# Three rounded products with the values, a second exponential on ScalarE, and a new order around the latent attention

## The reference, cut to what matters

```python
def mla_mixer(q_c, kv_c, k_r, pos, g_q, w_uq, g_kv, w_ukv):
    q = (rms_norm(q_c, g_q) @ w_uq).reshape(b, s, MLA_HEADS, MLA_QK)
    q = jnp.concatenate([q[..., :MLA_NOPE], rotary(q[..., MLA_NOPE:], pos)], -1)
    kv = (rms_norm(kv_c, g_kv) @ w_ukv).reshape(b, s, MLA_HEADS, MLA_NOPE + MLA_V)
    k_nope, v = kv[..., :MLA_NOPE], kv[..., MLA_NOPE:]
    ...
    return causal_block_attention(q, k, v)

def one_block(args):                      # inside causal_block_attention
    sc = jnp.einsum('bhqd,bhkd->bhqk', q_blk, kt, preferred_element_type=jnp.float32) * scale
    p = jax.nn.softmax(jnp.where(mask, sc, -jnp.inf), axis=-1)
    return jnp.einsum('bhqk,bhkd->bhqd', p.astype(vt.dtype), vt)
...
    a = mla_mixer(...)                    # in first_block
    r = retention_mixer(...)
    y = jnp.concatenate([a, r], axis=-1) @ w_out[l]
```

## Time and profile before

| | us |
|---|---|
| median of three runs | 2687.31 (2684.17 to 2688.14) |
| the profiled execution, its own time | 2691.6 |
| its span in the profile | 2689.8 |
| PE busy in the span | 2504.4 (93%) |
| DVE, ACT, POOL busy | 1350.4, 651.6, 733.9 |

### The profile page before, as it was taken

One profiled execution on the slowest core, in us unless ns is written; L12 is line 12 of the kernel. 1 busy time (PEld: TensorE's weight loads), 2 busy tenths in 40 slices (PEclk: granted clock), 3 DMA queues, 4 the chain that ended last, 5 costly groups with the idle time before them and its releaser, 6 DMA issues.

```text
span 2689.8 us, 29003 instructions
## 1 busy us (share of the span) xinstructions
PE 2504.4 (93%) x11544; PEld 1955.2 (73%) x11544; DVE 1350.4 (50%) x1513; ACT 651.6 (24%) x946; POOL 733.9 (27%) x490
## 2 busy tenths in 40 slices
PE   5998779989999999999998689999998999999998
PEld 3776556657678888888886368886586778888877
DVE  7556743434643444444435779996528321314433
ACT  3002224431432001101123421113204200025521
POOL 1241320015463332332345211210045223330011
PEclk9999879999999999999999899999999999979999
DMA  6651000022132332332222121112232521110021
GB/s 225 198 164 61 20 18 8 8 95 86 58 107 83 94 98 75 94 98 87 79 85 79 39 94 41 35 39 102 69 123 82 163 74 47 47 40 1 1 86 71
DMA packets 228851, 206.96 MB, mean 77 GB/s; under 512 B 15248, under 2 KB 203280, under 8 KB 227712
## 3 DMA queue, kind: packets, MB, share of 16 engines
q1 hardware_dynamic: 223552, 178.61, 21.9%
q10 hardware_dynamic: 3840, 21.89, 2.1%
q0 software_dynamic: 1344, 4.91, 0.5%
HBM read 180.35 MB, written 17.83 MB: 74 GB/s over the span
## 4 chain that ended last, share of the span: by engine, by line
PE 78%; DVE 9%; ACT 4%; issue 4%; PEld 2%; POOL 1%; DMA 1%; PEldq 1%; ACTq 0%; DVEq 0%; SPq 0%; POOLq 0%
PE G L1633 28%; PE G L304 25%; PE G L1099 2%; PE M L3001 2%; PE M L307 2%; PE G L2506 1%; PE M L400 1%; PE M L1649 1%; PE G L2322 1%; PE M L2322 1%; PE M L2986 1%; PE M L1010 1%; DVE WMAX L3024 1%; PE G L2349 1%; PE M L2508 1%
## 5 line engine op out<-in xcount | busy, mean ns | idle before, releaser
L278 POOL TENSOR_SCALAR WH<-RAW 128x1024 fp32r<-128x1024 f32 (+1 forms) x154 | 134.2, 872 | 887.2 <-PE G L1633 515.5
L304 PE MATMUL G<-HH,WH 128*128 128x512 f32 x1056 | 336.8, 400 | 14.5 <-POOL WL L2164 7.8
L304 PE MATMUL G<-HH,WL 128*128 128x512 f32 x1056 | 332.5, 396 | 0.0
L304 PE MATMUL G<-HL,WH 128*128 128x512 f32 x1056 | 332.4, 396 | 0.0
L281 POOL TENSOR_TENSOR WL<-RAW,WH 128x1024 fp32r<-128x1024 f32 (+1 forms) x154 | 299.4, 1944 | 12.9
L1633 PE MATMUL G<-HH,WH 128*128 128x512 f32 x640 | 227.2, 404 | 13.3 <-POOL WL L281 8.5
L304 PEld LDWEIGHTS G<-HH,WH 128*128 128x128 f32 x1056 | 188.2, 189 | 61.4 <-issue 19.2
L1633 PE MATMUL G<-HH,WL 128*128 128x512 f32 x640 | 223.8, 398 | 0.0
L1633 PE MATMUL G<-HL,WH 128*128 128x512 f32 x640 | 223.7, 398 | 0.0
L304 PEld LDWEIGHTS G<-HL,WH 128*128 128x128 f32 x1056 | 188.7, 188 | 42.2
L304 PEld LDWEIGHTS G<-HH,WL 128*128 128x128 f32 x1056 | 188.5, 188 | 42.1
(11 more groups left out here) (536 smaller groups left out, 4445.2 us busy)
## 6 DMA issues: line engine op xcount, KB each, us to landing
RAW<-in_w_ff SPq DMA_DIRECT2D x40, 512.0 KB, 3.8
RAW<-in_w_ff SPq DMA_DIRECT2D x80, 256.0 KB, 2.8
WVEC<-in_w_ada SPq DMA_DIRECT2D x24, 512.0 KB, 4.6
FVEC<-in_e_w_mod SPq DMA_DIRECT2D x24, 512.0 KB, 3.8
FVEC<-in_o_w_mod SPq DMA_DIRECT2D x24, 512.0 KB, 3.6
RAW<-in_o_w_in SPq DMA_DIRECT2D x24, 512.0 KB, 3.6
RAW<-in_e_w_in SPq DMA_DIRECT2D x20, 512.0 KB, 3.6
ADA<-in_w_ada SPq DMA_DIRECT2D x4, 2048.0 KB, 19.5
```

What stands on the lines that cost most here:

```text
L278: pool.tensor_scalar(hi, raw, 1.0, 0.0, ALU.mult, ALU.add).then_inc(w_high, 1)
L304: m = pe.matmul(G[s][:, n * w:(n + 1) * w], part[s][:, k, :], acts[i][:, k, n * w:(n + 1) * w], start=first, stop=last)
```

## The change

In the stage mla:

- The values become two float32r tiles, VPH (ACT) and VPL (DVE `v_low`). `values(g)` is three products: VPH and VPL against PH, and VPH against PL.
- ACT forms each exponential twice: PF in float32 (now three buffers), and PH in float32r (two buffers). DVE `p_low(g)` forms PL = PF - PH (three buffers). `scores(g)` waits for `ml_ph`, the second exponential of step g-2. The second exponential of step g waits for `ml_pv` of step g-2, that is for values(g-2), which read the same PH buffer.
- PE's order in step g is scores(g+1), largest(h+1, i), extras, values(g-2).
- The extras move: q_part to i=3 and k_part to i=6 in every even head, rows and chunks by a step or two; of the second group of rotated queries, one part stays in head 0 and one goes to head 1. The first pair's q_part and k_part become a lead in the stage ret, and the first v_part comes before the loop of maxima.
- DEN and NUM lie elsewhere, so that the weight buffers of units 0 and 1 are free by the end; POOL waits for the third pair's output (`ml_out` 3), then splits both. The lead of wf does both units: the second half of their rows, then the last pair's spread, then the first half.

Elsewhere: POOL begins win's splits only when DVE has finished the three chains (`ada_added`); the chain at the end of ret runs one head ahead; in ein POOL splits units 2 and 3 by itself; one of three loads in the stage odd is issued first. The diff at its core:

```diff
@@ -465,6 +467,8 @@
                     dve.wait_ge(S("ada_chain"), KT * i + k)
                     dve.scalar_tensor_tensor(out=acc, in0=ADA[g][:, k, c0:512], scalar=CACT[:, k:k + 1], in1=acc,
                                              op0=ALU.mult, op1=ALU.add).then_inc(S("ada_chain"), 1)
+            dve.wait_ge(S("ada_chain"), KT * len(CHAINS))
+            dve.sem_inc(ada_added, 1)
...
@@ -721,6 +725,7 @@
 
         def win_pool(pool):
             r0, u0 = info("win")["r0"], info("win")["u0"]
+            pool.wait_ge(ada_added, 1)
...
+            def gated(h):
                 dve.wait_ge(S("ret_t32"), h + 1)
                 dve.tensor_tensor(RG[:, h, :], T32R[h % 2][:], RG[:, h, :], ALU.mult).then_inc(S("ret_gate"), 1)
+
+            gated(0)
+            for h in range(RET_HEADS):
+                if h + 1 < RET_HEADS:
+                    gated(h + 1)
...
-        VP = Z("VPA", [P, NT, 192], F32, 0)
-        PF = [at(f"PF{i}", [P, 512], F32, (24 + 2 * i) * kb) for i in range(4)]
+        VPH, VPL = Z("VPH", [P, NT, 192], F32R, 0), Z("VPL", [P, NT, 192], F32R, 6)
+
+        PF, PL = [[at(f"{n}{i}", [P, 512], t, (24 + 2 * i) * kb) for i in range(3)] for n, t in (("PF", F32), ("PL", F32R))]
+        PH = [Z(f"PH{i}", [P, 512], F32R, 12 + 2 * i) for i in range(2)]
...
-        DEN = [at(f"DEN{i}", [P, 512], F32, (44 + 2 * i) * kb) for i in range(2)]
-        NUM0 = at("NUM0", [P, SEQ], F32, 52 * kb)
-        NUM = [NUM0, Z("NUM1", [P, SEQ], F32, 88), NUM0, Z("NUM3", [P, SEQ], F32, 124)]
+        DEN = [Z("DEN0", [P, 512], F32, 120), at("DEN1", [P, 512], F32, 30 * kb)]
+        NUM = [Z("NUM0", [P, SEQ], F32, 84), Z("NUM1", [P, SEQ], F32, 88), at("NUM2", [P, SEQ], F32, 52 * kb), Z("NUM3", [P, SEQ], F32, 124)]
...
+        def mla_first(pe):
+
+            q_part, k_part = mla_products(pe)
+            pe.wait_ge(mla_split, N_SPLIT)
+            pe.wait_ge(S("ret_dec"), NT)
+            pe.wait_ge(S("ret_state"), 2 * NT - 2)
+            q_part(G[0], WQN, 0, mla_lead)
+            k_part(G[1], 0, mla_lead)
...
-                need(pe, S("ml_e2"), g - 1)
+                need(pe, S("ml_ph"), g - 1)
...
-                        pe.wait_ge(S("ml_vhi"), h // 2 + 1)
-                pe.wait_ge(S("ml_e2"), g + 1)
-                first = 64 if h % 2 else 0
-                pe.matmul(G[1][:, cols_], VP[:, kb_, first:first + P], PF[g % 4][:, 0:n], start=(kb_ == 0),
-                          stop=(kb_ == 4 * c + 3)).then_inc(S("ml_pv"), 1)
...
+                        pe.wait_ge(S("ml_vlo"), h // 2 + 1)
+                pe.wait_ge(S("ml_plo"), g + 1)
+                first = 64 * (h % 2)
+                vh, vl = [v[:, kb_, first:first + P] for v in (VPH, VPL)]
+                pe.matmul(G[1][:, cols_], vh, PH[g % 2][:, 0:n], start=(kb_ == 0), stop=False)
+                pe.matmul(G[1][:, cols_], vl, PH[g % 2][:, 0:n], start=False, stop=False)
+                pe.matmul(G[1][:, cols_], vh, PL[g % 3][:, 0:n], start=False, stop=(kb_ == 4 * c + 3))\
+                  .then_inc(S("ml_pv"), 1)
...
                 if h % 2 == 0 and j + 1 < N_PAIR:
-                    if i == (1 if h else 4):
-                        take()
+                    if i == 3:
+                        take(pe)
                         q_part(M[1], WQN, j + 1, S("ml_qp"))
-                    if i == (3 if h else 6):
-                        take()
-                        k_part(M[1], j + 1)
+                    if i == 6:
+                        take(pe)
+                        k_part(M[1], j + 1, S("ml_kp"))
                 if h % 2 and j and i == 5:
-                    spread(j - 1)
+                    spread(pe, j - 1)
...
-            q_part(G[0], WQN, 0, S("ml_qp"))
-            k_part(G[1], 0)
+            v_part(0)
             pe.wait_ge(S("ml_rot"), 2)
             for n in range(NT):
                 largest(0, n)
-                if n == 0:
-                    v_part(0)
...
-                if g:
-                    values(g - 1)
-            values(len(STEPS) - 1)
-            spread(N_PAIR - 1)
+                if g > 1:
+                    values(g - 2)
+            for g in (2, 1):
+                values(len(STEPS) - g)
...
-            return (8, 10) if h == 0 else (7, 9)
+            return (7, 9) if h % 2 else (9, 11)
...
-            rope_high(0)
             q_high(0)
             k_high(0)
+            rope_high(0)
             v_high(0)
...
                 act.wait_ge(S("ml_s"), g + 1)
-                need(act, S("ml_pv"), g - 3)
-                act.activation(PF[g % 4][:, 0:n], src, ACT.Exp, scale=SCALE_M).then_inc(S("ml_e2"), 1)
+                need(act, S("ml_pv"), g - 2)
+                act.activation(PF[g % 3][:, 0:n], src, ACT.Exp, scale=SCALE_M).then_inc(S("ml_e2"), 1)
+                if g == 0:
+                    act.wait_ge(S("ml_kr"), 12)
+                need(act, S("ml_pv"), g - 1)
+                act.activation(PH[g % 2][:, 0:n], src, ACT.Exp, scale=SCALE_M).then_inc(S("ml_ph"), 1)
                 extras(h, g % N_STEP)
             chunk(MLA_HEADS - 1, 0)
...
+            def v_low(j):
+                dve.wait_ge(S("ml_vhi"), j + 1)
+                dve.tensor_tensor(VPL[:].rearrange("p t (a n) -> p t a n", a=3)[:, :, 0:3:2, :],
+                                  M[1][:].rearrange("p (t a n) -> p t a n", a=2, n=64),
+                                  VPH[:].rearrange("p t (a n) -> p t a n", a=3)[:, :, 0:3:2, :].bitcast(F32),
+                                  ALU.subtract).then_inc(S("ml_vlo"), 1)
+                dve.wait_ge(S("ml_vlo"), j + 1)
+                dve.sem_inc(S("ml_free"), 1)
+
+            def p_low(g):
+                n = step_cols(*STEPS[g][1:])[1]
+                dve.wait_ge(S("ml_e2"), g + 1)
+                dve.wait_ge(S("ml_ph"), g + 1)
+                dve.tensor_tensor(PL[g % 3][:, 0:n], PF[g % 3][:, 0:n], PH[g % 2][:, 0:n].bitcast(F32), ALU.subtract)\
+                   .then_inc(S("ml_plo"), 1)
+
...
+            q_low(0)
             rope_low(0)
-            q_low(0)
             k_low(0)
+            v_low(0)
             for n in range(NT):
                 smax(0, n)
             for g, (h, c, kb_) in enumerate(STEPS):
-                i, n = g % N_STEP, step_cols(c, kb_)[1]
+                i = g % N_STEP
+                p_low(g)
                 if i < NT and h + 1 < MLA_HEADS:
                     smax(h + 1, i)
...
+            pool.wait_ge(S("ml_out"), 3)
...
-                if i == 1:
+                if i == 2:
...
+            def products(s, k):
+                for part, moving in ((WH, HH), (WH, HL), (WL, HH)):
+                    m = pe.matmul(G[s][:, half(0)], part[s][:, k, :], moving[:, k, half(0)],
+                                  start=(k == 4 and part is WH and moving is HH), stop=(k == 3 and part is WL))
+                return m
+            for s in range(2):
+                pe.wait_ge(w_split[s], wf_U(s) // 2 + 1)
+                need(pe, unit_freed[s], wf_U(s) // 2)
+                if s:
+                    pe.wait_ge(S("ml_num"), 2 * MLA_HEADS)
+                for k in range(4, KT):
+                    products(s, k)
+            spread(pe, N_PAIR - 1)
+            for k in range(4):
+                pe.wait_ge(S("ml_out"), k + 1)
+                for s in range(2):
+                    m = products(s, k)
+                    if k == 3:
+                        m.then_inc(unit_done[s], 1)
...
-            if 2 <= i < 20:
+            if 4 <= i < 20:
...
-                if i < 2:
+                if i < 4:
...
-                    for dst, src in ((WC, "cos_win"), (WS, "sin_win"), (SWAPW, "swap_win")):
+                    for dst, src in ((SWAPW, "swap_win"), (WC, "cos_win"), (WS, "sin_win")):
```

More of the change, by code:

```diff
@@ L439, in start_sp @@
                   .then_inc(S(f"ada{g}"), 16)
+        ada_added = whole("ada_added")
         def start_dve(dve):
@@ L906, in ret_act, with scaled @@
             act.activation(SD[:], MV[:, :, 1], ACT.Sqrt, bias=vec("eps1"), scale=1.0).then_inc(S("ret_sd"), 1)
-            for h in range(RET_HEADS):
+            def scaled(h):
                 act.wait_ge(S("ret_nt"), h + 1)
@@ L912, in ret_act @@
                                scale=vec("gn_g", h)).then_inc(S("ret_t32"), 1)
+            scaled(0)
+            for h in range(RET_HEADS):
+                if h + 1 < RET_HEADS:
+                    scaled(h + 1)
                 act.wait_ge(S("ret_gate"), h + 1)
@@ L995, in passes, with take, mla_products @@
             return ((stationary[0], moving[0]), (stationary[0], moving[1]), (stationary[1], moving[0]))
-        def mla_pe(pe):
-            taken = [0]
-            def take():
-                need(pe, S("ml_free"), taken[0])
-                taken[0] += 1
+        mla_lead = whole("mla_lead")
+        taken = [0]
+        def take(pe):
+            need(pe, S("ml_free"), taken[0])
+            taken[0] += 1
+        def mla_products(pe):
             def q_part(dst, w, r, signal):
```

(36 more changed lines are left out.)

86 lines of the change are left out of this document (41 added, 45 removed).

## The result

The changed kernel takes 2878.6 us (2877.54 to 2880.95, four runs) against 2686.07 us before: ratio 1.0718, 95% interval 1.0699 to 1.0736. It is 192 us slower. The forecast was slower by 94, 2780 us, with 2735 to 2820 as its range: the right side, half the size. One of e5's four runs further down, at 2819 us, was in a slower state of the chip and is left out of its figures, so those rest on three. The profiled execution has a span of 2879.2 us.

The account below looks back on a forecast made before the run. PE was taken as the bound, so its microseconds per step and its waits count. Mla +108 (11 saved included), way in -10, end +3, start -1, ein -6: +94, about 2780 us, range 2735 to 2820.

Parts of the forecast that it names:

- The hand-off between PE and ACT: In mla's steps PE waits after each values product for the second exponential: 0.86 us at 512 columns, 9.0 a head.
- The chain through DVE: In heads 0 to 6, maxima wait behind p_low, which needs PH: steps i = 1 to 7 take 2.0 to 3.7 us.
- The sum: All terms added over the kernel: 108 - 10 + 3 - 1 - 6 = +94 us.
- The clock: PE in mla's steps: a loop with short gaps was taken to keep its clock level, read from two earlier stretches.
- a rival with 17%: Clock falls and stays in even heads: some 13 steps +1.1 us each, up to 15 in three pairs, 2795 to 2825; 17%.
- a granted clock of 0.5 over tens of us: Sign named ahead that would show the forecast wrong and the falling-clock rival, chance 17%, right.
- The saving of the passes: Values in mla: three passes of 0.24 us replace 0.92, saving 0.20 per 512-column step, 11 us over 96 steps.
- The way into mla: Before mla's first scores: ret's chain -4 us, moved q_part, k_part and v_part -6, so -10 (-4 to -14).
- The start: Kernel start: third chain about 3.5 us without POOL's splits instead of 8.32, but delayed splits meet later steps; -1 taken.
- The end: After the last values: unit 2's load and split come as late, PE idle where unit 1 lay; +3 taken (0 to +5).
- The way into ein: PE's 7.80 us wait for POOL's split of unit 2 falls to about 3: -6 us (0 to -7).
- PE busy in the stage near two thirds: Sign named ahead that would show the forecast right: PE's busy share in mla.

Follow-up runs that it names:

- e5: e4 with one stricter wait on ScalarE: the exponential of step g waits for the product of step g-1, not g-4; 2771.6 us, ratio 1.0321.
- e1: Changed kernel with the product with the values ahead of scores(g+1) in TensorE's step instead of at its end; 2709.2 us, ratio 1.0086.
- e10: e3 without the four useless products ahead of the maxima, so only the gap behind the values is filled; 2812.8 us, ratio 1.0464.
- e2: Changed kernel with the row maximum ahead of the subtraction p_low on VectorE; 2839.3 us, ratio 1.0553.
- e3: Changed kernel with useless products in TensorE's gaps, behind the values and ahead of six blocks of maxima; 2807.2 us, ratio 1.0449.
- e4: Changed kernel with the old steps (one exponential, one float32 product, no low parts), its other edits kept; 2663.9 us, ratio 0.9911.
- e7: e1 without the subtraction p_low, the third pass taking other operands of the same size; 2683.2 us, ratio 0.9983.
- e8: Kernel before with one edit in ein: GpSimd forms the high parts of units 2 and 3, ScalarE from unit 4; 2679.6 us, ratio 0.9977.

## Why the prediction was right in its direction and wrong in its size

By its own steps:

- **The hand-off between PE and ACT.** Right: 0.84 us measured for 0.86 in one step, and PE waited there in 88 of 96. e1 shows the cause, the place of the values in PE's row.
- **The chain through DVE.** There, but smaller than summed in the kernel as it ran. A step measured at full clock took 3.55 for 3.4 us. The sum had 4.5 us a head for the chain, 31 us in seven heads; in the changed kernel PE waited 10.2 us for maxima, and in e10, at a clock of 0.86, 20.8. Taking the chain away (e2) shortened the steps by 30 us, and that this is the sum's 31 is luck: 7 of the 30 are idle time, and the rest is clock.
- **The clock, the step that failed.** "So a loop with short gaps keeps what level it has" was read from two stretches of the earlier trace rows, 12 us at 1.2 GHz and 9 us at 2.4 GHz, the second with 4.01 us busy. This put the half clock into a rival with 17%, confined to 13 steps in each of three pairs, 15 us a pair, and left it out of the sum. So the forecast priced PE's own work in the steps at full clock. In the changed kernel the clock was 0.60 over all 96 steps and four pairs. PE was busy 129 us more there, where the sum had 11 less. The rival's sign of being right ("a granted clock of 0.5 over tens of us") came, and its 2795 to 2825 was still too low. Its term was right per step: "+1.1 each" by the text; head 5, at a clock of 0.57, took 49.0 us from its first scores to those of head 6, against 32.2 and 2.0 for its spread in the sum, 1.2 a step. Its count was wrong, nearly all of the 96 instead of some 39. e3 prices it: a clock of 0.90 again is worth 71 us although PE does more. The remaining 25 us between e3's 345 and the sum's 320 are partly clock too (0.90) and partly waits; that is not separated.
- **The saving of the passes.** 0.23 to 0.24 a pass, as taken. No run shows the 11 us as a gain, since each version with three passes was slower than e4: PE was busy 196.3 us in e7's steps and 192.9 in e4's, at clocks of 0.93 and 0.96.
- **The way into mla.** The first scores came 9.4 us earlier, for 11 with the start's 1.'s wait of 8.83 is 4.3.
- **The start.** 54.34 before, 53.38 after for the first product of win: -0.96 for -1. The third chain, whose additions read two SBUF tiles, took 8.32 us beside GpSimd's splits and 3.61 without them (3.5 expected). That is what the rule of the Trainium skill cited ahead (SBUF — State Buffer, Who interferes with whom) says, and the trace agrees. The modulation behind the chain rose from 1.53 to 3.64 us for two, now beside GpSimd's splits. It reads one tile and a column of scalars, so the rule on two inputs, by which the forecast had it held back, does not cover it, though the trace shows it held back.
- **The end.** GpSimd's split of the fifth unit of wf began 31.1 us after the last values before (613.37 - 582.3) and 33.5 after (810.08 - 776.56): +2.4 for +3.
- **The way into ein.** 7.80 to 2.81: -5.0 for -6, and e8 measures the edit alone at -2 to -10.

Outside the steps the sum had -14 and the trace has -14.3 (189.4 - 203.7, by the spans). The error is in the 96 steps: 203.7 for 108. The forecast's sign "PE busy in the stage near two thirds" missed for the same reason: it was 324.8 of 415.6 us, 78%, since at half clock PE's own work fills time in which it was to stand.

## What to carry to other kernels

A stall of PE that comes in every step costs twice where the clock follows: count it once as idle time, and once as PE's own time at half clock over the whole loop (here 129 us more busy time beside 75 us more idle time). So where a new order gives an engine in lockstep a gap per step, price the loop at both clocks before choosing. The cure may be one line: put between the release of a buffer and its next use a whole step of other work; failing that, products that nobody needs, which here won back 71 of 192 us.

Before an arithmetic is made cheaper on the engine that bounds, count what it adds to the engines beside it: here an expected 11 us on TensorE were bought with 54 us of VectorE (79.6 to 133.9) and 38 of ScalarE (91.9 to 130.4).

## What the runs showed of the hardware that was not expected

- Gaps of about 0.7 us in steps of 3.5 to 5 us, with a few of 1 to 2.5 in even heads, went with a clock of 0.59 in a middle pair, though PE was busy 85 of its 109 us. In the kernel before, at 49.5 of 54.4 us, the clock was 0.97. The stretch of the earlier trace rows with 4.01 of 9 us busy and a clock of 1.00 was no guide to this loop.
- 373 products more (e3 against the changed kernel) made the kernel 71 us faster.
- Two of the kernels scatter with the same instructions each time: e5's three times spread over 28 us and e2's four over 34, while those of the changed kernel, e3 and e4 lie within 3.4 to 5.5. The clock changes level within the steps of the changed kernel too, so what sets the spread is not shown.
